# Hybrid mixer of a two-part transformer block: three rotations ahead of the stick projection, ScalarE's gate copies behind the next exponential, weight splits one step later

## The reference

```python
def hybrid_mixer(h, positions, w_in, b_fgate, ...):
    proj = h @ w_in                      # 1024 x 6774, in f32
    fox_qkv, fox_f, dsa_qkv, idx_q, idx_k, idx_w, sb_qkv, gates = split(proj)
    # 6 "fox" heads: softmax(q k * scale + c_q - c_k, causal), c = cumsum(log_sigmoid(fox_f + b))
    # 5 "dsa" heads: q and k rotated (rope); each query attends only to its top 64 keys by
    #    score = sum_h relu(rope(idx_q_h) . rope(idx_k)) * idx_w_h
    # 5 "stick" heads: a = exp(log_sigmoid(z) + cumsum from the right of log_sigmoid(-z)), no softmax
    g = sigmoid(gates)                   # three gates of 256 x 1024
    merged = g0 * (o_fox @ w_fox_out) + g1 * (o_dsa @ w_dsa_out) + g2 * (o_sb @ w_sb_out)
    return merged @ w_out
```

## Time and profile before

| | us |
|---|---|
| three runs, median (lowest to highest) | 2761.64 (2759.4 to 2762.7) |
| the profiled execution's own time | 2763.96 |
| its span in the profile | 2761.8 |
| first mixer, from its stick projection to the last gates | about 1497 to 1667 |
| second mixer, the same stretch | about 2255 to 2430 |

### The profile page before, as it was taken

The page is one execution under the profiler, slowest core; times in us unless marked ns, Lnnn a source line. Parts: engine busy times, 40 slices in busy tenths (PEclk is TensorE's granted clock), DMA queues, the critical chain, the costliest instruction groups (busy, mean ns, idle before and its releaser), DMA issues.

```text
span 2761.8 us, 44768 instructions
## 1 busy us (share of the span) xinstructions
PE 2604.4 (94%) x18413; PEld 2338.9 (85%) x18413; DVE 1732.5 (63%) x3255; ACT 1261.6 (46%) x2246; POOL 176.7 (6%) x211
## 2 busy tenths in 40 slices
PE   6999988999989989999999989999999999899998
PEld 3676567888868689999999879899999998798998
DVE  4565946454575566677654877776665548676764
ACT  3443634223255554454444445554544444455543
POOL 1000000000033410000000010000000000100001
PEclk8999999999989999999999999999999999999999
DMA  8655522322325325556555324465665553244664
GB/s 262 193 181 184 179 96 77 106 92 92 107 80 119 77 94 168 167 162 179 167 174 161 123 69 159 125 184 166 195 189 163 171 158 122 69 146 129 178 169 121
DMA packets 515818, 397.02 MB, mean 144 GB/s; under 512 B 26024, under 2 KB 491184, under 8 KB 515616
## 3 DMA queue, kind: packets, MB, share of 16 engines
q1 hardware_dynamic: 512816, 388.02, 46.6%
q0 software_dynamic: 2080, 3.53, 1.0%
q10 hardware_dynamic: 720, 2.62, 0.2%
HBM read 393.08 MB, written 1.05 MB: 143 GB/s over the span
## 4 chain that ended last, share of the span: by engine, by line
PE 80%; DVE 11%; ACT 4%; issue 2%; DMA 1%; POOL 1%; SPq 0%; DVEq 0%; ACTq 0%
PE pv L746 41%; PE pa L746 30%; PE pv L711 5%; DVE Wl L1839 3%; PE pa L711 2%; ACT Wh L1359 2%; DMA ring<-in_w_mod_dram 1%; PE pa L870 1%; PE pa L716 1%; DVE Lb L1991 1%; POOL Pb L2476 1%; DVE T L1912 0%; DVE HTl L1846 0%; DVE T L1911 0%; ACT Pb L1455 0%
## 5 line engine op out<-in xcount | busy, mean ns | idle before, releaser
L1839 DVE TENSOR_TENSOR Wl<-ring,Wh 128x1024 fp32r<-128x1024 f32 (+4 forms) x688 | 765.6, 1153 | 332.8 <-ACT Wh L1359 330.1
L1359 ACT ACTIVATE Wh<-ring 128x1024 fp32r<-128x1024 f32 (+4 forms) x688 | 647.8, 990 | 450.9 <-PE pv L746 445.5
L746 PE MATMUL pa<-HTl,Wh 128*128 128x256 f32 (+2 forms) x1648 | 537.9, 326 | 41.3 <-DVE HTl L1931 24.0
L746 PE MATMUL pv<-HTl,Wh 128*128 128x256 f32 (+1 forms) x1872 | 546.5, 292 | 17.9 <-DVE Wl L1839 6.3
L746 PE MATMUL pv<-HTh,Wl 128*128 128x256 f32 (+1 forms) x1872 | 537.6, 287 | 0.0
L746 PE MATMUL pv<-HTh,Wh 128*128 128x256 f32 (+1 forms) x1872 | 537.3, 287 | 0.0
L746 PE MATMUL pa<-HTh,Wl 128*128 128x256 f32 (+2 forms) x1648 | 522.7, 317 | 0.0
L746 PE MATMUL pa<-HTh,Wh 128*128 128x256 f32 (+2 forms) x1648 | 521.8, 317 | 0.0
L746 PEld LDWEIGHTS pv<-HTl,Wh 128*128 128x128 f32 x1872 | 359.5, 192 | 33.3 <-DVE Wl L1839 8.8
L746 PEld LDWEIGHTS pa<-HTl,Wh 128*128 128x128 f32 (+1 forms) x1648 | 321.6, 195 | 75.0 <-issue 44.9
L746 PEld LDWEIGHTS pv<-HTh,Wl 128*128 128x128 f32 x1872 | 360.0, 192 | 2.7 <-issue 0.2
(11 more groups left out here) (237 smaller groups left out, 3944.5 us busy)
## 6 DMA issues: line engine op xcount, KB each, us to landing
ring<-in_ffn_w_gu_dram SPq DMA_DIRECT2D x176, 512.0 KB, 5.1
ring<-in_w_mlp_dram SPq DMA_DIRECT2D x64, 1024.0 KB, 5.2
ring<-in_w_in_dram SPq DMA_DIRECT2D x54, 1024.0 KB, 5.2
ring<-in_w_mod_dram SPq DMA_DIRECT2D x48, 1024.0 KB, 6.0
ring<-in_ffn_w_down_dram SPq DMA_DIRECT2D x64, 704.0 KB, 4.6
ring<-in_a_w_qkv_dram SPq DMA_DIRECT2D x12, 1024.0 KB, 5.3
ring<-in_b_w_qkv_dram SPq DMA_DIRECT2D x12, 1024.0 KB, 5.2
ring<-in_w_out_dram SPq DMA_DIRECT2D x8, 1024.0 KB, 5.1
```

The costliest lines, as they stand in the source:

```text
L746: m = nc.tensor.matmul(o, lhsT=x, rhs=y, start=first and j == 0, stop=last and j == 2)
L1359: ins = nc.scalar.activation(Wh[rows, p % SPLIT, a:b], ring[rows, i % RING, a:b], ACT.Copy)
L1839: ins = v.tensor_tensor(Wl[rows, p % SPLIT, a:b], ring[rows, i % RING, a:b], Wh[rows, p % SPLIT, a:b].bitcast(F32), ALU.subtract)
```

## The change

Three things move; no arithmetic is added or removed.

1. `TURNS = ((0, 3), (3, 6), (6, 9), (9, 11))` replaces the groups of four: three rotations (`iq` 0 to 2) come before the first stick block on TensorE, then three, three and two behind the blocks. On VectorE the first three come before the `prepare()` that stood first in the loop.
2. In the attention stage ScalarE's copy of a gate tile (and the two late groups of the index relu) moves from the end of step i to step i+1, behind that step's exponential and in front of the copy of T. ScalarE's `prepare()` moves with it to the end of step i+1. So in the program before ScalarE goes: exponential, T, gate, `prepare()`; now: exponential, gate, T, stick, `prepare()`.
3. VectorE's `prepare()` beside the gates and the two late index sums come one step later (`gate_tile(i - 2)` for `gate_tile(i - 1)`).

```diff
@@ constants
+TURNS = ((0, 3), (3, 6), (6, 9), (9, 11))
@@ TensorE, mixer
+                for key, n, x in turns[slice(*TURNS[0])]:
+                    rotate(key, n, x)
                 for j, offsets in enumerate(((0, P), (0, HEAD), (0, P))):
                     linear(A, (("sb", l), "qk"), 2 * j, offsets, hx, S)
...
-                    for key, n, x in turns[4 * j:4 * j + 4]:
+                    for key, n, x in turns[slice(*TURNS[j + 1])]:
                         rotate(key, n, x)
@@ ScalarE, mixer
-                def beside(i):
-                    if i < 2:
-                        index(l, 3 + i)
-                    stick(i - STICK_FROM)
-                    j = gate_tile(i)
+                def gate_of(i):
+                    if 1 <= i < 3:
+                        index(l, 2 + i)
+                    j = gate_tile(i - 1) if i else None
                     if j is not None:
                         copy((("g", l), j), G[:, j, :], lambda b: b[:, 0:S])
-                        if j % 2:
-                            prepare()
+
+                def beside(i):
+                    stick(i - STICK_FROM)
+                    j = gate_tile(i - 1) if i else None
+                    if j is not None and j % 2:
+                        prepare()
...
-                attention(("mix", l, "att"), "mix", units("mix"), after=beside)
-                for i in range(len(units("mix")) + 2, MIX_STEPS):
+                attention(("mix", l, "att"), "mix", units("mix"), gate_of, beside)
+                for i in range(len(units("mix")) + 2, MIX_STEPS + 1):
+                    gate_of(i)
                     beside(i)
@@ VectorE, mixer
+                def turned(first, end):
+                    for key, n, x in turns[first:end]:
+                        dve.wait_ge(a_free, A.nth((key, n)))
+                        rotated(x, x.shape[0], (key, n, "r"), C("cos"), C("sin"), wide_queries(key, n))
+
+                turned(*TURNS[0])
                 for j in range(3):
                     prepare()
                     if j == 0:
                         copy_in(("cum", l), cum, lambda b: b[:, 0:S])
                         dve.wait_ge(v_free, V.nth(("cum", l)))
-                    for key, n, x in turns[4 * j:4 * j + 4]:
-                        dve.wait_ge(a_free, A.nth((key, n)))
-                        rotated(x, x.shape[0], (key, n, "r"), C("cos"), C("sin"), wide_queries(key, n))
+                    turned(*TURNS[j + 1])
...
                 def beside(i):
-                    if i < 2:
-                        index(3 + i)
+                    if 1 <= i < 3:
+                        index(2 + i)
...
-                    j = gate_tile(i - 1) if i else None
+                    j = gate_tile(i - 2) if i >= 2 else None
                     if j is not None and j % 2:
                         prepare()
...
-                for i in range(len(units("mix")) + 3, MIX_STEPS):
+                for i in range(len(units("mix")) + 3, MIX_STEPS + 1):
                     beside(i)
```

## The result

The changed kernel took 2742.56 us (median of four runs, 2739.37 to 2743.62), the kernel before on the same chip 2762.17 (four runs, 2759.4 to 2765.01). The ratio is 0.9907, 95% interval 0.989 to 0.9925: 21 to 30 us faster. The forecast of 2747.5 had taken off 14.1 us and saw too small a gain. The two medians themselves are only 19.6 apart, which lies outside that interval, and the record doesn't show why. Both kernels once more, further down, were 28.2 apart. The profiled execution of the changed kernel took 2739.37, its span is 2737.2. The two spans, 2761.8 and 2737.2, are 24.6 apart.

The account below looks back on a forecast made before the run. TensorE is busy 94% of the span, but VectorE sets the pace from 1505 to 1532. Per mixer -5.3 + 1.0 - 2.7 = -7.0, twice -14.0, off the median 2761.64 gives 2747.5 us; range 2740 to 2756.

Parts of the forecast that it names:

- The clock is open: TensorE's clock left out of the sum: fewer stick-step waits could give 1 to 3 us a mixer, new waits take as much.
- the clock stays up as well: Rival: TensorE's clock also stays at its upper level, 3 us more a mixer, 2741.5 us; chance 0.15.
- Rotations, -5.3: Before the first stick block: three early rotations fill VectorE's idle time, so the index sum starts 5.3 us earlier a mixer.
- the half clock behind 1508: TensorE's lower clock behind the wait for the copy of `cum`: counted inside the rotations' 5.3 us, not on top.
- Splits, +1.0: Attention gates: VectorE's later split makes gate 4 some 1.6 us late; about 1.0 us a mixer stays lost.
- the 0.6 that I let come back: Gates behind gate 4: 0.6 of the 1.6 us delay regained in small waits TensorE has had there.
- 0.5 of slack: Gate 10 and further on: the later VectorE split is just in time, with 0.5 us to spare.
- Copies and rounding, -2.7: Stick steps from 12 on: ScalarE's gate copy behind the exponential shortens `PT` waits, 0.46 + 1.1 + 1.14 us a mixer.
- the -14.0 of the sum: Both mixers: rotations, splits and gate copies, -5.3 + 1.0 - 2.7 = -7.0 us a mixer, twice.
- 1 to 3 us a mixer back: Stick steps: clock gain that fewer TensorE waits could bring, not counted in the sum.
- the new waits at gates 1 and 4: Attention gates: two new TensorE waits that could cost as much clock as the 1 to 3 us a mixer regained.
- GpSimd's product: Stick head 0: taken as 1.09 us instead of 2.00, since the split no longer runs beside it; not in the sum.

Follow-up runs that it names:

- fillers: Kernel before in its old order, with overwritten matmuls added where TensorE would wait (rotations, steps 16 and 20): 2751.11 us, ratio 0.9947.
- split_back: Changed kernel with VectorE's splits back in their old place, one step earlier; ScalarE's order stays as changed: 2746.9 us, ratio 0.9927.
- mixed_fill: Changed kernel with splits in their old place up to step 13 and overwritten matmuls before running sums of stick heads 0, 1, 3, 4: 2735.68 us, ratio 0.9882.
- before_again: Kernel before once more, unaltered, for a second profile: 2769.63 us.
- mixed12_fill: Changed kernel with splits in their old place up to step 11 and overwritten matmuls before running sums of stick heads 1, 3, 4: 2735.74 us, ratio 0.9877.

## Why the prediction was too small

The direction was right, and so were the three places and the waits that go or come there. The step that failed is the sentence "The clock is open", and what hung on it: beyond the one fall inside the rotations' 5.3 the sum held only the waits and counted the clock at nothing, and the case "the clock stays up as well" got a chance of 0.15. The runs showed 9.3 us of clock in its place between the first two profiles, and more between others.

- **Rotations, -5.3.** Measured -5.43, and the wait for `RQ` is gone. The remark that the half clock behind 1508 is part of the 5.3 holds: by fillers it is 1.5 of it. (The row of 1.46 us holds the three rotations alone, without `cum`; the stick block began 0.42 later, not 0.6.) But there was a second fall, in the stick values (it began at 1535.57), that I hadn't priced, though the mean clock of 0.94 over 54.5 us is 3.3 us lost and so two falls; it is gone as well, in all profiles of kernels with early rotations but one. That makes gate 0 6.7 earlier and not 5.4. Why it is gone stays open, since the wait beside it stays: 1.66 us for `TMP`, in the old order and in the new. In the old order a wait of 0.78 ended 3.1 us ahead of that one's end, and a fall came in all eight mixers profiled; in the new one the wait before it is 8.9 us away, and a fall came in 1 of 20.
- **Splits, +1.0.** Gate 4 waits 0.91 for its split and is 1.6 late, as said. At gate 12 1.45 of it is left: the 0.6 that I let come back did so up to gate 7, but small waits grew at gates 8 and 10, where I had seen 0.5 of slack, and at gate 12 only 0.15 of the 0.6 was left. And the split isn't only a loss, as the prediction had it: without it the stick steps take 60.3 instead of 56.5 (split_back).
- **Copies and rounding, -2.7.** Gates 12 to 20 without falls take 59.18 in the old order (fillers) and 56.49 in the new: -2.69. Inside it 1.0 is the copy's and 1.7 that of the rounding with its split. The size came out right while the sum of it was put together wrongly: copy and rounding alone, without the later split that stood there only as a loss, would have made the stretch 1.1 longer than the old order's 59.2.
- **The three terms together** are thus -5.43 + 1.45 - 2.69 = -6.67 a mixer, -13.3 against the -14.0 of the sum. Of it some 3.0 is the clock behind the wait for `RQ`, so plain waits make 10.3.
- **The clock beyond that** is the rest. The fall in the stick values gives 1.3 a mixer. Behind gate 12 the kernel before lost 8.5 us in one profile and 15.4 in the other, the changed one 1.7 and 0. So 13.3 + 2.5 + 6.8 = 22.6 between the first two profiles, which is what the milestones show (9.6 + 13.0), and up to 31 between others. The prediction said "1 to 3 us a mixer back"; measured, between the first profiles, 1.7 and 5.1 behind gate 12, and the 1.3 besides. What I feared, that the new waits at gates 1 and 4 take as much, shows in no profile: between gates 0 and 12 the clock is 1.00 in all of them. All in all the clock is 12.3 of the 22.6, which fits the page: TensorE busy for 12 us less.
- **The remaining 2 us** of the 24.6 between the spans lie outside the mixers (4.1 less ahead of the first, 2.2 more between them), where both kernels are the same. The clock fell at other places there: its cost ahead of the first mixer is 5.1 less, between the mixers 3.4 more. It varies between profiles of one kernel too: the transpose came at 1492.48 and at 1494.72 in the changed one.
- **GpSimd's product** took 1.09 for head 0, as taken, now that no split runs beside it. By the rule that the prediction took from the Trainium skill (SBUF — State Buffer, Who interferes with whom) a normalisation could hold the product. That rule is for a VectorE instruction with two SBUF inputs, and the normalisation reads one tensor, `Pb`, and a number a row. In the trace it is the normalisation that gives way. Of VectorE and GpSimd in the changed kernel:

```profile
1592.68 0.35 DVE L2009 TENSOR_SCALAR Pb<-Pb,rr 128x256 f32<-128x256 f32 x1
...
1597.49 1.00 DVE L2009 TENSOR_SCALAR Pb<-Pb,rr 128x256 f32<-128x256 f32 x1
```

```profile
1597.25 1.09 POOL L2515 TENSOR_TENSOR BIG<-BIG,con 128x512 f32<-128x512 f32 x1 [183.12 <-DVE BIG L2327]
```

The product began 0.24 us earlier and kept its 1.09; the normalisation took 0.65 longer than alone. The same section of the Trainium skill says that whoever issues first holds the port and the other fully blocks. The trace agrees on who gives way; a full block would have made it 0.85 + 0.35 = 1.2, and it took 1.00. In the kernel before, the split began first, 0.16 us ahead of the product, and there both took 0.9 longer: the product 2.00, the split 3.25 instead of 2.36:

```profile
1606.87 3.25 DVE L1839 TENSOR_TENSOR Wl<-ring,Wh 128x1024 fp32r<-128x1024 f32 x2
```

That idling of TensorE brings falls is shown by fillers: nine falls of the first profile became two, both where nothing was filled, and its five runs lost 16.8 us less to the clock than the kernel before beside it (in the profiles 16.5, of them 12.0 in the mixers). mixed_fill (three became none) points the same way with one profile each. Not shown is why a given wait brings one in one profile and none in another. In the changed kernel a wait of 1.78 was followed by a fall in one mixer, and by none in the other and in the second profile. The Trainium skill (TensorE: Matmul & The Clock Gate, What's actually happening) says that the gate looks at activity on its own time, which doesn't start with the kernel; that would fit, and no run here was made to test it.

## What to carry to other kernels

Where the profile shows a stretch with a clock below 1.00, work out what the clock costs there (the sum of length x (1 - clock) by slices) in every stage that the edit touches, and put it into the sum as a term with its own chance; here it was 12.3 us against 10.3 of plain waits. Read the granted clock of every run, and not of the profiled one alone. Compare two kernels by length less busy time in a fixed stretch of work first: it repeats to 0.03 us, while the time of one execution moves by 10 with the falls. And when an instruction is moved behind others on one engine, the partner that waits for it on the next engine has to move with it: the later split was a loss by itself and still right beside the later rounding.

## What the runs showed of the hardware

- A fall of TensorE's clock came in steps: some 3.4 us at the lower level, 1.7 us of work lost, in all 14 profiles. In the two mixers of these profiles there are 41 stretches at the lower level, and at each of them a wait of TensorE of 0.61 to 2.35 us ended between 1.7 us before the start of the stretch and 0.5 us behind it. Several can follow one another: 10.2 us lost within 69 in the second mixer of before_again.
- The same kernel has them in different number, with identical waits: 8.5 and 15.4 us behind gate 12. Runs of the kernel before range from 2759.4 to 2775.16 over the chips used. Whether an order with few waits is steadier isn't shown: beside each other, seven runs of the kernel before range over 5.1 us and four of mixed_fill over 2.4, but four of mixed12_fill range over 12.4.
- 12 matmuls a mixer whose results are overwritten made the old order 0.5% faster (0.9947, 0.9929 to 0.9965).
- A VectorE split and a GpSimd product of 1.09 us that overlap cost each other 0.9 us when the split begins first; a normalisation of 0.35 that begins 0.24 behind the product takes 1.00.
